# A transformer block on one core: the last half tile of the keys is projected in steps 52 to 55, and the end regime of the attention begins at step 56

## The reference

```python
h = rmsnorm(x, g_pre_mix)
proj = einsum('bsd,de->bse', h, w_in) + b_in
aq, ak, av, bq, bk, bv = split(proj)
out_a = mixer_a(...)   # 8 query heads, 2 key heads, window of 128, sinks, T5 bias
out_b = mixer_b(...)   # 8 heads of 64; chunks of 64 see their own and 8 former chunks, bias by distance
y = concatenate([out_a, out_b]) @ w_out
x = x + rmsnorm(y, g_post_mix)
h = rmsnorm(x, g_pre_mlp)
u = square(relu(h @ w_up))
x = x + rmsnorm(u @ w_down, g_post_mlp)
```

## Time and profile before

| what | value |
|---|---|
| median of 3 runs | 1037.47 us (1037.4 to 1037.55) |
| the profiled execution | 1037.82 us |
| its span, first to last instruction | 1036.0 us |
| TensorE busy | 1026.4 us, 99% |
| DVE, ScalarE, GpSimd busy | 771.1, 467.8, 214.9 us |
| mean granted TensorE clock | 0.998 |

### The profile page before, as it was taken

One profiled execution on the slowest core, in us unless ns is written; L12 is line 12 of the kernel. 1 busy time (PEld: TensorE's weight loads), 2 busy tenths in 40 slices (PEclk: granted clock), 3 DMA queues, 4 the chain that ended last, 5 costly groups with the idle time before them and its releaser, 6 DMA issues.

```text
span 1036.0 us, 15823 instructions
## 1 busy us (share of the span) xinstructions
PE 1026.4 (99%) x5555; PEld 854.0 (82%) x5555; DVE 771.1 (74%) x1505; ACT 467.8 (45%) x961; POOL 214.9 (21%) x200
## 2 busy tenths in 40 slices
PE   9999999999999999999999999999999999999997
PEld 7899887788777888888888888888888888888886
DVE  5855678766679478889988788786444777778997
ACT  5532255554478477846131121221344444444562
POOL 0400000000000003148676675672100000000000
PEclk9999999999999999999999999999999999999999
DMA  9454552110062365135444434436777733454344
GB/s 250 118 134 131 120 134 62 49 65 22 27 183 84 101 184 163 41 127 208 173 168 158 170 128 160 163 133 215 252 240 240 242 95 99 138 193 142 97 139 167
DMA packets 123894, 147.92 MB, mean 143 GB/s; under 512 B 56976, under 2 KB 74264, under 8 KB 121768
## 3 DMA queue, kind: packets, MB, share of 16 engines
q1 hardware_dynamic: 123128, 146.71, 44.8%
q10 hardware_dynamic: 688, 0.20, 0.1%
HBM read 103.65 MB, written 47.49 MB: 146 GB/s over the span
## 4 chain that ended last, share of the span: by engine, by line
PE 96%; issue 1%; DVE 1%; ACT 1%; DMA 0%; SPq 0%; DVEq 0%; ACTq 0%
PE ps L2163 28%; PE ps L2165 28%; PE ps L2164 28%; PE ps L2376 3%; PE ps L2362 2%; PE ps L2343 2%; PE ps L2287 1%; PE ps L2322 1%; PE ps L2495 1%; PE ps L2497 1%; PE ps L2483 1%; PE ps L2175 1%; DMA xraw<-in_x 0%; PE ps L2513 0%; PE ps L2300 0%
## 5 line engine op out<-in xcount | busy, mean ns | idle before, releaser
L2164 PE MATMUL ps<-tm_lo,sm_hi 128*128 128x512 f32 (+1 forms) x450 | 174.6, 388 | 0.0
L2165 PE MATMUL ps<-tm_hi,sm_lo 128*128 128x512 f32 (+1 forms) x450 | 174.6, 388 | 0.0
L2163 PE MATMUL ps<-tm_hi,sm_hi 128*128 128x512 f32 (+1 forms) x450 | 174.6, 388 | 0.0
L2163 PE MATMUL ps<-b_hi,wc_hi 128*128 128x512 f32 x448 | 174.6, 390 | 0.0
L2165 PE MATMUL ps<-b_hi,wc_lo 128*128 128x512 f32 x448 | 174.3, 389 | 0.0
L2164 PE MATMUL ps<-b_lo,wc_hi 128*128 128x512 f32 x448 | 174.3, 389 | 0.0
L1419 ACT ACTIVATE sm_hi<-sm_raw 128x512 fp32r<-128x512 f32 x112 | 70.7, 631 | 162.0 <-DMA sm_raw<-u_matrices 162.0
L2067 DVE TENSOR_TENSOR sm_lo<-sm_raw,sm_hi 128x512 fp32r<-128x512 f32 x112 | 77.7, 693 | 78.3 <-ACT sm_hi L1419 77.7
L2165 PEld LDWEIGHTS ps<-tm_hi,sm_lo 128*128 128x128 f32 x450 | 84.5, 188 | 17.5
L2163 PEld LDWEIGHTS ps<-tm_hi,sm_hi 128*128 128x128 f32 x450 | 84.5, 188 | 17.5
L2163 PEld LDWEIGHTS ps<-b_hi,wc_hi 128*128 128x128 f32 x448 | 84.1, 188 | 17.8 <-DVE wc_lo L1839 0.3
(11 more groups left out here) (239 smaller groups left out, 2062.4 us busy)
## 6 DMA issues: line engine op xcount, KB each, us to landing
u_matrices<-stage SPq DMA_DIRECT2D x112, 256.0 KB, 2.0
sm_raw<-u_matrices SPq DMA_DIRECT2D x112, 256.0 KB, 2.6
up_raw<-in_w_up SPq DMA_DIRECT2D x16, 1024.0 KB, 5.0
w<-in_w_down SPq DMA_DIRECT2D x64, 256.0 KB, 3.7
w_raw<-in_w_in SPq DMA_DIRECT2D x8, 512.0 KB, 3.4
xr<-in_x SPq DMA_DIRECT2D x8, 512.0 KB, 4.7
x_rows<-xr SPq DMA_DIRECT2D x8, 512.0 KB, 5.5
xf<-x_rows SPq DMA_DIRECT2D x8, 512.0 KB, 3.5
```

Source lines behind the costliest of these rows:

```text
L2163: pe.matmul(out, w_hi_, x_hi_, start=start, stop=False)
L2164: pe.matmul(out, w_hi_, x_lo_, start=False, stop=False)
L2165: return pe.matmul(out, w_lo_, x_hi_, start=False, stop=stop)
```

## The change

The last half tile (8 triples) is no longer made in steps 52 and 53 with 4 triples each, but with 1, 2, 2 and 3 triples in steps 52 to 55. `LATE` goes from 54 to 56, and the rotation of the banks begins at step 55 and no longer at 53. The scores of step 56 wait for 25 low halves instead of 26; step 60, the first whose keys reach into the last half, waits for the 26th. `WO_STEPS` and SyncE's program are unchanged.

```diff
-LATE = 54
+LATE = 56
+
+ROTATED = 55
+
+LAST_FILLS = {52: 1, 53: 2, 54: 2, 55: 3}
...
-    return min(168 + 4 * (n - 31), 8 * HALVES)
+    held = 8 * HALVES - sum(LAST_FILLS.values())
+    return min(168 + 4 * (n - 31), held) + sum(v for m, v in LAST_FILLS.items() if m <= n)
...
-            if n >= LATE - 1:
+            if n >= ROTATED:
                 bank = (6, 4, 5)[(len(banks) + A_STEPS // 2) % 3]
...
                 if t == 0:
-                    pe.wait_ge(s_elo, (14, 18, 22, 26)[p - 4])
+                    pe.wait_ge(s_elo, (14, 18, 22, 25)[p - 4])
+                elif n == STEPS - 4:
+                    pe.wait_ge(s_elo, 26)
...
-                first, end = min(filled(n - 1), 8 * HALVES), filled(min(n, STEPS - 1))
+                first, end = filled(n - 1), filled(min(n, STEPS - 1))
```

## The result

| | before | changed |
|---|---|---|
| median of 14 runs | 1037.44 us | 1040.03 us |
| lowest and highest | 1037.11, 1038.44 | 1038.74, 1041.17 |
| the profiled execution, its span | 1037.82, 1036.0 | 1040.29, 1038.5 |

The ratio is 1.0022, with a 95% interval of 1.0014 to 1.0030: slower by 2.6 us in the medians. The spread grew as well, from 1.3 to 2.4 us. In the changed kernel's trace step 52 starts at 282.31 and not at 282.72 as in the earlier trace rows, so instants from here on stand 0.41 us lower than the forecast ones. That lies ahead of the change: in the profiles of the experiments step 52 starts anywhere from 281.94 to 282.66. Where it matters, times are therefore counted from the start of step 52, or the 0.41 is added.

The account below looks back on a forecast made before the run. TensorE, busy 99% of the span, was taken as the bound. The closed gap (−0.3) and new stalls (+0.7) were contained in the late exponential, leaving +3.3 us on the median 1037.47: 1040.8 us, range 1038.6 to 1042.6.

Parts of the forecast that it names:

- No idle time to fill in 54 and 55: TensorE is busy in all of steps 54 and 55 (3.56 and 3.63 us), so added work fills no gap there.
- The last fill at 301.5: TensorE's last fill matmul, before at 293.60, ends at 301.5, with 0.7 us of new stalls in steps 53 to 55.
- ScalarE at the load at 305.4: In step 56 ScalarE reaches block 0's high part at 305.4 and waits 2.4 us there for its load.
- Block 0 lands 6.3 us after the last fill: SyncE's load of weight block 0 takes the same 6.3 us after the last fill as before, landing at 307.8.
- The slack of 4.3 us: Before the change, block 0 landed 4.3 us ahead of ScalarE's use of it; the change eats this slack.
- The estimate of 3.2 us: By the skill's fit, block 0 lands 3.2 us after the last fill, at 304.7, before ScalarE comes: no wait.
- What hangs on the wait, and what keeps it: Exponentials of 57 come 3.4 us late, DVE's scores of 58 3.3 us late; no slack behind absorbs it.
- Rival B: TensorE's hole of 2.9 us before step 57's transposes drops its clock to 1.2 GHz: 1042 to 1043 us, chance 0.10.
- The new stalls are contained in the late exponential: The 0.7 us of new stalls in steps 53 to 55 lie ahead of the late exponential, adding nothing to +3.3.
- DVE's added work costs nothing: Tile 25's scaling and low part (0.75 us), moved to steps 56 and 57, fall into DVE's wait for the exponentials.
- Rival A: Block 0's load lands in time for ScalarE; exponentials of 57 only 1.0 us late: 1038.5 us, chance 0.12.
- Rival C: Gaps of step 56 and some behind it close without a new wait: 1037.1 us; chance 0.06 with all smaller sums.

Follow-up runs that it names:

- run 10: The changed kernel timed again unaltered, on the same chip as run 8 and run 9: 1039.31 us.
- run 1: Changed kernel with the high parts of weight blocks 0 and 1 made in steps 58 and 59 instead of 56 and 58: 1037.90 us.
- run 7: Changed kernel with high parts of blocks 0 and 1 in steps 58 and 59, and step 53's chunks in banks 5, 6, 5: 1037.43 us.
- run 6: Changed kernel in which SyncE waits for both halves of weight block 0 before issuing the other ten loads: 1039.54 us.
- run 4: Changed kernel with the fills as before (4 triples in steps 52 and 53), only regime and bank rotation beginning two steps later: 1041.18 us.
- run 3: Changed kernel with twelve extra transposes of a constant in TensorE's hole ahead of step 57's first chunk: 1038.98 us.
- run 9: Changed kernel with weight loads issued only after step 57's scores, plus 38 extra transposes of a constant in TensorE's hole: 1043.16 us.
- run 8: Changed kernel with the weight loads issued only after the scores of step 57, 3.5 us later: 1044.59 us.
- run 2: Kernel before the change, with only SyncE's loads of the output weights waiting for the scores of step 56: 1039.08 us.

## Why the prediction was right, and where not

Forecast were 1040.8 us with 1038.6 to 1042.6, measured 1040.03. The mechanism was right and its size was not; a rival that I had held for unlikely made up for most of the difference. That the number came so near is luck: with the wait as it was and the full clock, the forecast's own sum gives 1040.8 − 1.4 = 1039.4, which is what run 10 measured (1039.31). The prediction took 0.2% for the least that a measurement can tell; the interval here reaches 0.08% to either side and is clear of 1.

- *No idle time to fill in 54 and 55.* Right. Even with the load out of the way the change gains nothing (runs 1 and 7).
- *The last fill at 301.5.* Measured 301.29, or 301.70 with the offset. The stalls were 0.58 + 0.23 = 0.81 where I took 0.7, at the two places named, the first through bank 6.
- *ScalarE at the load at 305.4.* Measured 304.50 + 0.72 = 305.2, or 305.6.
- *Block 0 lands 6.3 us after the last fill.* This is the term that was mis-sized: 4.9 in the first profile. I read it from one execution, in which the second half took 5.7 us. In the changed kernel it took 4.3, and in the profiles of the experiments 4.0 to 4.9, mostly 4.1. The wait was 1.0 and not 2.4 us. The slack of 4.3 us is of that one execution too: with 4.9 it is 5.7, and the fill's shift of 8.1 less ScalarE's own of 1.4 less 5.7 is the wait of 1.0. Why that half took 5.7 once is open; its followers do not explain it by run 6, and its place does not by run 4, whose loads start as early as those of before and whose second half took 4.1. The estimate of 3.2 us from the Trainium skill ("DMA: Bandwidth & Descriptors", section "Anatomy of one DMA — SWDGE (gpsimd) path"), whose fit is for transfers that GpSimd issues and not SyncE, errs on the other side: the two halves were never there before 4.6 us, even with no followers (0.6 + 4.0), and its case, no wait, did not come.
- *What hangs on the wait, and what keeps it.* Right, one for one: runs 3 and 9. DVE's scores of 58 came 1.91 us late, forecast 3.3; the 1.4 less are the 1.4 of the wait. Behind them nothing is absorbed: the table below has the same lateness at the output stage wherever the clock stayed up.
- *Rival B, the clock.* I gave it 0.10, since no row of before showed a fall and the hole of 2.9 us seemed short. It fell behind a smaller one, 1.39 us by TensorE's timeline, with only 0.54 us busy in the two windows from 307 to 309. That is the other wrong step. Its price of 1 to 2 us was a little high: 0.85 in the changed kernel's trace, 1.2 behind the hole of 5.48 us (8 minus 9). The Trainium skill ("TensorE: Matmul & The Clock Gate", section "HAM oscillation — how this bites in real kernels") says that idle gaps throw the array back to the half clock. Run 8's trace agrees: the clock fell within its hole of 5.48 us and is 0.50 from 312 to 316. But the gaps of which the section speaks are longer than the changed kernel's hole, so the fall behind 1.39 us does not follow from it.
- *The new stalls are contained in the late exponential.* Right as long as the load is late, since they delay the last fill. Without that wait they appear: run 7 puts the one of step 53 at 0.5 us.
- *DVE's added work costs nothing.* Right even without the cover of the wait: run 7 has that work and is level with before.
- *Rival A* (in time, 1038.5) did not come. Run 1 is not quite its picture, since it moves the high part as well; run 3 less its wait, 1038.98 − 0.8 = 1038.2, is an estimate of it. *Rival C* did not come.

How late two marks are against before, counted from the start of step 52, in us, by the timelines:

| | DVE's scores of 58 | output stage's first low product | clock below 1.00 between them |
|---|---|---|---|
| changed kernel | 1.91 | 2.76 | yes |
| 10, the same again | 1.70 | 1.71 | no |
| 3 | 1.68 | 1.70 | no |
| 2 | 1.30 | 1.31 | no |
| 1 | 0.58 | 0.59 | no |
| 7 | 0.13 | 0.14 | no |
| 8 | 5.98 | 7.09 | yes |
| 9 | 5.77 | 5.77 | no |

The balance by the medians: 0.5 for the stalls of step 53 (1 minus 7), 1.1 for the wait and the high part of block 0 together (3 minus 1), 0.3 to 1.0 for the clock (10 or the first 14 runs minus 3), together 1.9 to 2.6, the two results of the changed kernel. It must close, as each term is the step from one kernel to the next. Of the 1.1, 0.8 is the wait in run 3's profile, and some 0.3 is left for the high part, an estimate. What stays open is how often the clock falls in the changed kernel, and what else spreads the times of runs 3 and 6.

## What to carry to other kernels

Before moving the last reader of a buffer, look for the load that overwrites it and for the first instruction that wants that load: the slack between them (4.3 us in one profile here, 5.7 with the landing that the changed kernel's had) is in no table of waits, and a shift beyond it turns into a stall on an in-order engine with everything queued behind. Take the landing time of a transfer from several profiles: one gave 6.3 us from the first issue to the second landing where others gave 4.6 to 5.5. And a hole in a matmul engine that is busy 99% of the time can have two prices, the hole and the slow stretch behind it: here 0.85 us behind a hole of 1.39, 1.2 with one of 5.48, and nothing behind one of 1.20. Before an experiment moves an instruction to take a wait away, count what the instruction itself took: run 1 moved 1.0 us of work with the wait.

## What the runs showed of the hardware

- The granted clock fell to 0.50 of 2.4 GHz, that is 1.2 GHz, after TensorE had waited 1.39 us in one execution, and stayed at 1.00 after 1.20 us in another (run 10) and after 1.23 us in run 2. It was back at 1.00 within 314 to 315 in the first. In run 4 it was 0.50 in the window 306 to 308 after several stalls, the longest 1.15 us.
- With transposes of a constant in the hole the clock stayed at 1.00 in run 9, where without them (run 8) it was 0.50 from 311 to 317: worth 1.2 us. It stayed at 1.00 in run 3 as well, but in run 10 it did so without them.
- The slow stretch of the changed kernel's profile, 3.4 us at half clock, cost 0.85 us at the output stage.
- The same 256 KB load, second in its queue, landed 4.0 to 5.7 us after its issue, mostly 4.1.
